# A third expert weight buffer and 32-row tiles in the mixture-of-experts half of a fused decoder layer

## What is computed

```python
x = x + g1 * y                                  # after the mixer: "x2" in the kernel
h = rms_norm(x, norm_ffn) * (1 + sc2) + sh2
x = x + g2 * hier_moe(h, ...)                   # "x3" in the kernel
return rms_norm(x, final_norm)
...
# hier_moe: 4 groups of 4 experts; each token takes the top group and the top 2 experts in it
g_top  = top_k(softmax(t @ w_rg + b_rg), 1)
e_top  = top_k(softmax(logits_e of that group), 2)
for each expert:                                # w_gate, w_up: 1024 x 512, w_down: 512 x 1024
    hid = silu(t @ w_gate) * (t @ w_up)
    y  += combine[:, expert] * (hid @ w_down)
```

## Time and profile before

| | |
|---|---|
| median of 3 runs | 833.36 us (833.19 to 833.53) |
| the profiled execution, its own time | 836.89 us |
| its span in the trace | 835.2 us |
| PE busy | 702.7 us, 84% of the span |
| DVE, ACT, POOL busy | 335.3, 177.6, 131.2 us |
| moved by DMA | 173.49 MB, mean 208 GB/s |

### The profile page before, as it was taken

How to read it: one execution, slowest core, us unless ns; L and a number is a source line. 1 busy time by engine, 2 the same in 40 slices (tenths; PEclk the granted TensorE clock), 3 DMA queues, 4 the chain that set the end, 5 groups by cost and what they waited for, 6 DMA issues and landing times.

```text
span 835.2 us, 8861 instructions
## 1 busy us (share of the span) xinstructions
PE 702.7 (84%) x3377; PEld 397.4 (48%) x3377; DVE 335.3 (40%) x743; ACT 177.6 (21%) x427; POOL 131.2 (16%) x171
## 2 busy tenths in 40 slices
PE   0469899999999998889999815999998999899920
PEld 0455445667675796555544513444443344334300
DVE  4932566866575434867221174011211111021107
ACT  3203225121121213557121201111211112011103
POOL 8650022313050281000000001000000000000021
PEclk9669999999999998989999855999999999999975
DMA  9899802222220305510520422489999999999935
GB/s 335 262 312 276 288 0 101 101 102 101 101 101 1 53 1 192 191 73 2 202 94 19 168 97 64 165 281 401 374 388 396 381 399 383 399 369 397 398 110 230
DMA packets 88092, 173.49 MB, mean 208 GB/s; under 512 B 19347, under 2 KB 23533, under 8 KB 88045
## 3 DMA queue, kind: packets, MB, share of 16 engines
q1 hardware_dynamic: 78048, 151.12, 50.8%
q0 software_dynamic: 4240, 15.21, 5.6%
q10 hardware_dynamic: 5756, 6.52, 2.3%
HBM read 157.63 MB, written 15.20 MB: 207 GB/s over the span
## 4 chain that ended last, share of the span: by engine, by line
PE 66%; DVE 14%; DMA 12%; ACT 3%; issue 2%; POOL 1%; SPq 0%; ACTq 0%; POOLq 0%; DVEq 0%
PE ps L962 14%; DMA gu<-in_w_up 10%; PE ps L1067 7%; PE ps L2107 6%; PE ps L2074 5%; PE ps L955 3%; PE ps L989 3%; DVE acc L1733 3%; PE ps L2185 2%; PE ps L2191 2%; PE ps L2071 2%; PE ps L983 2%; PE ps L2098 2%; PE ps L2195 2%; PE ps L636 1%
## 5 line engine op out<-in xcount | busy, mean ns | idle before, releaser
L962 PE MATMUL ps<-gu,xgT 128*128 128x512 f32 x256 | 117.0, 617 | 8.3 <-DMA gu<-in_w_up 5.9
L962 PEld LDWEIGHTS ps<-gu,xgT 128*128 128x128 f32 x256 | 49.9, 198 | 70.5 <-issue 63.7
L1401 POOL DMA_INDIRECT xg<-xn_rows,list x16 | 15.0, 940 | 413.1 <-PE ps L943 221.2
L2107 PE MATMUL ps<-hT,winr 128*128 128x512 f32 x144 | 72.1, 609 | 0.0
L1733 DVE SCALAR_TENSOR_TENSOR acc<-ada,st,acc 128x512 f32<-128x512 f32 x84 | 68.1, 811 | 2.3
L1067 PE MATMUL ps<-wout,yT 128*128 128x512 f32 x128 | 58.6, 617 | 0.0
L955 PE MATMUL ps<-gu,xgT 128*64 128x512 f32 x256 | 56.7, 595 | 0.0
L989 PE MATMUL ps<-dn,hidT 128*128 128x512 f32 x128 | 56.5, 594 | 0.0
L1038 DVE TENSOR_TENSOR hidm<-sg,ps 128x512 f32<-128x512 f32 x8 | 5.5, 686 | 121.6 <-ACT sg L1005 121.6
L1587 POOL TENSOR_TENSOR cc<-low,lev 128x512 f32<-128x512 f32 x20 | 30.2, 1520 | 129.7 <-DVE low L1919 104.2
L2074 PE MATMUL ps<-hT,wind 128*128 128x512 f32 x96 | 42.3, 593 | 0.0
(11 more groups left out here) (401 smaller groups left out, 1041.9 us busy)
## 6 DMA issues: line engine op xcount, KB each, us to landing
gu<-in_w_gate SPq DMA_DIRECT2D x16, 2048.0 KB, 14.6
gu<-in_w_up SPq DMA_DIRECT2D x16, 2048.0 KB, 20.5
dn<-in_w_down SPq DMA_DIRECT2D x16, 2048.0 KB, 20.5
ada<-in_w_ada SPq DMA_DIRECT2D x12, 2048.0 KB, 10.4
expert_rows<-zero POOLq DMA_DIRECT2D x9, 512.0 KB, 10.8
expert_rows<-yo ACTq DMA_DIRECT2D x8, 512.0 KB, 6.7
wout<-in_w_out SPq DMA_DIRECT2D x1, 3072.0 KB, 10.7
x<-in_x SPq DMA_DIRECT2D x2, 1024.0 KB, 6.2
```

The costliest lines, as they stand in the source:

```text
L962: ins = nc.tensor.matmul(PS[2 * b + w][:, :], T["xgT"][:, k, :], gu[b][:, w, k, :], start=(k == 0), stop=(k == KT - 1))
L2107: ins = t.matmul(bank[:, :], w(k), T["hT"][:, k, :], start=(k == 0), stop=(k == KT - 1))
```

## The change

- A third pair of weight buffers, `gu2` and `dn2`. `gu2` lies over the old x, xn2, x2T, `g1b`, `g2b` and `fnb`, and `dn2` over x2. Experts 0, 1 and 2 are now pinned, and step n uses buffer n % 3.
- x2 is therefore stored to a DRAM tensor `x2_rows` after the output projection (4 stores of 512 KB) and loaded again near the end as `x3` (2048 KB), over `dn1`. `fnb`, the final norm's gains, is loaded near the end too.
- g2 is copied to places of its own (`g2m`, `g2s`, `g2q`) by ACT, ahead of the routing's two exponentials; before, DVE made `g2s`, after the routing.
- The tiles are now 8 of 128 rows, 4 of 64 and 4 of 32. In a 32-row tile four products of 32 rows run side by side, each against a quarter of the weights' columns (moving size 256), with their results in four groups of 32 partitions.
- The order of ranks is now 0, 1, 2, 15, 3, 14, 4, 13, 5, 12, 6, 11, 7, 8, 9, 10.
- `EXTRA` goes from 9 to 12, with as many DRAM tiles zeroed by POOL near the start. Several semaphores of the routing are merged into one that counts.

```diff
-EXTRA = 9
-BIG = 8
-HALF = 64
+EXTRA = 12
+NBUF = 3
+SIZES = [128] * 8 + [64] * 4 + [32] * 4
...
     at("x2", R1 + 64 * K + 256, [P, ST, D])
+    at("dn2", R1 + 64 * K + 256, [P, FT, D])
+    at("x3", RW + 16 * K, [P, ST, D])
...
+    at("gu2", RX, [P, 2, KT, F])
...
-    ORDER = [0, 1]
-    for m in range(BIG - 2):
-        ORDER += [BIG + m, 2 + m]
-    ORDER += [E - 2, E - 1]
+    ORDER = list(range(NBUF))
+    big, less = list(range(NBUF, BIG)), list(range(BIG, E))
+    rest = less[::-1] if NBUF == 3 else less
+    while big:
+        ORDER.append(rest.pop(0))
+        ORDER.append(big.pop(0))
+    ORDER += rest[::-1] if NBUF == 3 else rest
@@ sync_moe
-        sp.dma_start(T["fnb"][:], A["final_norm"].partition_broadcast(P)).then_inc(sem("fn_in"), 16)
-        sp.wait_ge(sem("experts"), 1)
+        for i in range(ST):
+            sp.dma_start(x2_d[i * P:(i + 1) * P, :], T["x2"][:, i, :]).then_inc(sem("x2_st"), 16)
+        sp.wait_ge(sem("g2_moved"), 1)
+        sp.wait_ge(sem("ss"), 2 * ST)
+        sp.wait_ge(sem("logit_mm"), ST)
+        for b in range(2):
+            sp.wait_ge(sem(f"xn2_st{b}"), 32)
+        load_gate_up(sp, 2, 2)
+        sp.wait_ge(sem("x2_st"), 16 * ST)
+        load_down(sp, 2, 2)
+        sp.wait_ge(sem("routing"), ROUTING["experts"])
...
-        for n in range(2, E + 1):
+        for n in range(NBUF, E + 1):
...
-                sp.wait_ge(sem("gu_mm"), n - 1)
-                load_gate_up(sp, expert[n], n % 2)
-            if n >= 3:
-                sp.wait_ge(sem("dn_mm"), n - 2)
-                load_down(sp, expert[n - 1], (n - 1) % 2)
+                sp.wait_ge(sem("gu_mm"), n - NBUF + 1)
+                load_gate_up(sp, expert[n], n % NBUF)
+            if n > NBUF:
+                sp.wait_ge(sem("dn_mm"), n - NBUF)
+                load_down(sp, expert[n - 1], (n - 1) % NBUF)
+        sp.wait_ge(sem("gu_mm"), E - 1)
+        sp.dma_start(T["fnb"][:], A["final_norm"].partition_broadcast(P)).then_inc(sem("fn_in"), 16)
+        sp.wait_ge(sem("dn_mm"), E - 2)
+        sp.dma_start(T["x3"][:], x2_d.rearrange("(i p) d -> p i d", p=P)).then_inc(sem("x3_in"), 16)
@@ pe_gate_up, a tile of fewer than 128 rows (pe_down alike)
+            parts = P // m
+            f = F // parts
             for k in range(KT):
-                for s in range(2):
+                for s in range(parts):
                     ins = nc.tensor.matmul(
-                        PS[2 * b][HALF * s:HALF * s + HALF, :].rearrange("p (w f) -> p w f", w=2),
-                        T["xgT"][:, k, 0:HALF], gu[b][:, :, k, s * GW:(s + 1) * GW], start=(k == 0),
-                        stop=(k == KT - 1))
+                        PS[2 * b][m * s:m * s + m, 0:2 * f].rearrange("p (w f) -> p w f", w=2),
+                        T["xgT"][:, k, 0:m], w_in[:, :, k, s * f:(s + 1) * f], start=(k == 0), stop=(k == KT - 1))
@@ act_moe, ahead of the exponentials
+        act.wait_ge(sem("oproj_mm"), ST)
+        act.wait_ge(sem("ada_out"), HPS - 4)
+        for name, m in (("g2m", P), ("g2s", 64), ("g2q", 32)):
+            d = D * m // P
+            for s in range(P // m):
+                ins = a.activation(T[name][m * s:m * s + m, :], T["g2b"][m * s:m * s + m, s * d:(s + 1) * d], ACT.Copy)
+        ins.then_inc(sem("g2_moved"), 1)
@@ dve_moe, in the routing
-        link(v.tensor_scalar(t16, order, -float(BIG), 0.0, ALU.add, ALU.max))
         link(v.tensor_scalar(tile0, order, float(P), None, ALU.mult))
-        v.scalar_tensor_tensor(tile0, t16, -float(P - HALF), tile0, ALU.mult, ALU.add)
-        link(v.tensor_scalar(pad, order, BIG - 0.5, float(P - HALF), ALU.is_gt, ALU.mult))
+        for m, n in enumerate(STEPS_DOWN):
+            less = float(SIZES[n - 1] - SIZES[n])
+            link(v.tensor_scalar(t16, order, -float(n), 0.0, ALU.add, ALU.max))
+            link(v.scalar_tensor_tensor(tile0, t16, -less, tile0, ALU.mult, ALU.add))
+            if m:
+                link(v.tensor_scalar(t16, order, n - 0.5, less, ALU.is_gt, ALU.mult))
+                link(v.tensor_tensor(pad, pad, t16, ALU.add))
+            else:
+                link(v.tensor_scalar(pad, order, n - 0.5, less, ALU.is_gt, ALU.mult))
...
-        link(v.scalar_tensor_tensor(e16[:], rank, float(HALF), pad.unsqueeze(1).broadcast_to([P, ST, E]), ALU.is_ge,
-                                    ALU.mult))
+        wide_pad = pad.unsqueeze(1).broadcast_to([P, ST, E])
+        link(v.tensor_tensor(e16[:], rank, wide_pad, ALU.add))
+        link(v.scalar_tensor_tensor(e16[:], e16[:], float(P), wide_pad, ALU.is_ge, ALU.mult))
...
-        v.tensor_copy(T["g2s"][0:HALF, :], T["g2b"][0:HALF, 0:512])
-        v.tensor_copy(T["g2s"][HALF:P, :], T["g2b"][HALF:P, 512:1024])
@@ dve_moe, at the end
         dve.wait_ge(sem("fn_in"), 16)
+        dve.wait_ge(sem("x3_in"), 16)
```

More of the change, by code:

```diff
@@ L48 @@
 FT = F // P
-EXTRA = 9
-BIG = 8
-HALF = 64
-TILE_START = [P * n for n in range(BIG)] + [P * BIG + HALF * n for n in range(E - BIG)]
-TILE_START += [P * BIG + HALF * (E - BIG) + P * n for n in range(EXTRA)]
+EXTRA = 12
+NBUF = 3
+ROUTING = {"chosen": 1, "places": 2, "slots": 3, "list": 4, "experts": 5, "w12": 6, "route_i": 7}
+ROUTING_PE = {"rank_mm": 1, "list_mm": 2}
+SIZES = [128] * 8 + [64] * 4 + [32] * 4
+TILE_START = [sum(SIZES[:n]) for n in range(E + 1)]
+TILE_START += [TILE_START[E] + P * (n + 1) for n in range(EXTRA - 1)]
 ROWS = TILE_START[-1] + P
+BIG = SIZES.count(P)
+STEPS_DOWN = [n for n in range(1, E) if SIZES[n] < SIZES[n - 1]]
 EPS = 1e-6
@@ L940, in pe_rows @@
             pe.wait_ge(sem("xgT_d"), n)
-        m = HALF if small(n) else P
+        m = rows_of(n)
         for k in range(KT):
@@ L968, in pe_hidden, with pe_down @@
         pe.wait_ge(sem("hidm"), n + 1)
-        for f in range(2 if small(n) else FT):
+        for f in range(FT * rows_of(n) // P):
             ins = nc.tensor.transpose(PS[2 * b][:, f * P:(f + 1) * P], T["hidm"][:, f * P:(f + 1) * P], idf[:])
         ins.then_inc(sem("hid_tr"), 1)
-    def pe_down(pe, n, b, came):
+    def pe_down(pe, n):
+        w_in = dn[buffer_of(n)]
         pe.wait_ge(sem("hidT"), n + 1)
-        pe.wait_ge(sem(f"dn_in{b}"), came)
+        pe.wait_ge(sem(f"dn_in{buffer_of(n)}"), 16 * loads_of(n))
         pe.wait_ge(sem("yo_d"), n + 1)
+        m = rows_of(n)
         if small(n):
+            parts = P // m
+            per = FT // parts
+            d = D // parts
             for f in range(FT):
[L981 to L984, removed]
-                                           dn[b][:, f, w * 512:(w + 1) * 512], start=(f == 0), stop=(f == FT - 1))
+                s, c = f // per, f % per
+                for w in range(parts):
+                    ins = nc.tensor.matmul(PS[4][m * w:m * w + m, 0:d], T["hidT"][:, c, m * s:m * s + m],
+                                           w_in[:, f, w * d:(w + 1) * d], start=(f == 0), stop=(f == FT - 1))
         else:
@@ L1016, in act_output @@
         start = TILE_START[ORDER[n] if n < E else n]
-        rows = yo_d[start:start + (HALF if small(n) else P), :]
-        if small(n):
-            for s in range(2):
-                act.dma_start(rows[:, s * 512:(s + 1) * 512], T["yo"][HALF * s:HALF * s + HALF, 0:512]
-                              ).then_inc(sem("yo_st"), 16)
-        else:
-            act.dma_start(rows, T["yo"][:]).then_inc(sem("yo_st"), 16)
+        m = rows_of(n)
+        d = D * m // P
+        for s in range(P // m):
+            act.dma_start(yo_d[start:start + m, s * d:(s + 1) * d], T["yo"][m * s:m * s + m, 0:d]
+                          ).then_inc(sem("yo_st"), 16)
     def dve_rows(dve, n):
         dve.wait_ge(sem("xg_tr"), n + 1)
-        m = HALF if small(n) else P
+        m = rows_of(n)
         for k in range(4, KT):
@@ L1135, in pe_moe @@
                                start=(n + i == 0), stop=(n == 1 and i == ST - 1))
-        ins.then_inc(sem("list_mm"), 1)
-        pe.wait_ge(sem("list"), 1)
+        ins.then_inc(sem("routing_pe"), 1)
+        pe.wait_ge(sem("routing"), ROUTING["list"])
         pe_rows(pe, 0, 0, 16)
-        pe_gate_up(pe, 0, 0, 32)
+        pe_gate_up(pe, 0, 0)
         pe_rows(pe, 1, 1, 16)
@@ L1392, in pool_moe @@
         at = bass.IndirectOffsetOnAxis
-        pool.wait_ge(sem("list"), 1)
+        pool.wait_ge(sem("routing"), ROUTING["list"])
         for b in range(2):
@@ L1530, in _ @@
         link(g.tensor_scalar(T["pinned"][:], T["e1"][:], -1.0, float(E - 1), ALU.mult, ALU.add))
-        for e in range(2):
-            link(g.memset(T["pinned"][:, e:e + 1], (2 - e) * 1e6))
+        for e in range(NBUF):
+            link(g.memset(T["pinned"][:, e:e + 1], (NBUF - e) * 1e5))
         pool.wait_ge(sem("masks"), 1)
```

105 lines of the change are left out of this document (62 added, 43 removed).

## The result

The changed kernel takes **823.42 us** (median of 4 runs, 822.75 to 825.09) against 833.44 (833.19 to 835.39) for the kernel before on the same chip: a ratio of 0.9865 (95% interval 0.9834 to 0.9895), 10.0 us less. The forecast was 817.5 in a range of 812 to 826: the direction and the range held, and in the main the mechanism, and the gain is 10 us where 15.9 were forecast. The profiled execution of the changed kernel took 824.05 us, with a span of 822.1, against 836.89 and 835.2 before.

A forecast was written before the change was run, and what follows sets the result against it. Before the change DMA and PE were full together, after it the weights' stream alone; 793.4 - 19.6 + 1.6 + 1.2 = 776.6 for the last down load, last down ending at 784.2, execution 821.0, median 817.5 us, range 812 to 826.

The forecast's parts named there:

- first rival: 32-row steps: four products side by side don't overlap, a step costs 11.4 us, PE stays full; about 826, chance 0.05.
- The account of bytes: Weights' stream: 98.8 MB before, 91.2 MB after, 7.6 MB less, at 388 GB/s 19.6 us less.
- The late loads: Loads of x2, gu2 and dn2 before the first gather: if late, they share its engines, 0 to 3 us; 0 taken.
- The other rivals: Holes in the stream, about 828 (0.07); slower clock after waits, about 847 (0.04); a spare tile used, about 856 (0.01).
- A change that relieves one of the two gains almost nothing: Expert loop before the change: DMA and PE are full together, so relieving only one gains almost nothing.
- check of PE's chain for the kernel before: PE's step times summed from 516.0 with eight steps of 11.6 and its waits give 800; its last down ended at 800.5.
- The stretch to the last gate/up: From the first load into a freed buffer to the last gate/up's start: 19.4 us less.
- The new hole: Stream: step 5's load waits for a 128-row gate/up until 570.4 us; costs about 1.6 us, bounds 0 and 5.
- Step 0: Routing chain ahead of step 0 and the stream's start: more linked operations, 1.2 us more.
- The last gate/up: Last gate/up to end of last down: 16.5 us before, 1.9 us added for the clock's fall after a wait.
- The 32-row step: PE's work on a 32-row tile: 1.9 + 1.0 + 1.0 for transposes, 3.9 us a step, other bound 11.4.
- Waits in nearly every pair: Expert loop: PE waits some 10 us for weights per pair of a 128- and a 32-row expert; a sign of being right.

The follow-up runs named there:

- The buffer alone: The changed kernel with tiles of 8 x 128 and 8 x 64 rows as before; third buffer, x2 through memory and order stay: 826.88 us, ratio 0.9897.
- second execution: The changed kernel run again with no edit, against the kernel before on the same chip: 823.72 us, ratio 0.9868.
- the three kernels with the other order: The changed kernel with 32-row tiles in the last two steps: 820.97 us; with gate half freed early and spare tiles' work later: 816.32; plus useless products: 817.21.

## Why the prediction was right, and where 6 us went

**What held, and what the number owes to luck.** 823.4 lies in the forecast's own range of 813 to 824, but nearer to the first rival's 826 than to 817.5; the time alone would not have told the two apart. The traces do: a 32-row gate/up takes 3.66 us and not 7, and PE has slack. The account of bytes said that the weights' stream would bound the kernel alone. The DMA share is 1.04 to 781 us with PE busy for 93% of the time, and taking 4.2 MB away brought the last gate/up 11.1 us forward, for the 10.7 us that they need. The late loads are out too: `xg` of step 0 was there 4.4 us after its gather was issued, and 5.4 before. The other rivals are out: 32-row steps are cheap, no load after 576 us came late enough to open a hole, the waits did not halve the clock for long, and there were 16 steps.

**"A change that relieves one of the two gains almost nothing" was wrong.** The buffer alone gains 8.6 us. Both resources were full on average, but PE lost time at particular places, in waits for weights and slow stretches behind them, and in that run these are gone. That it is the 6.3 MB loaded ahead that removes them, and not the third place or the order, is likely but not shown. The forecast's own rival had this sum in it (about 826, PE full without waits), and 826.88 is what the buffer alone gives; the general sentence above it ignored it. In the check of PE's chain for the kernel before, the forecast's named terms give 796.4; only with those two slow stretches of 1.7 us each do they reach the 800 that it states.

**The stretch to the last gate/up: -15.1 for -19.4.** This is the term that was mis-sized, by 4.3 us.
- The new hole was foreseen at its place (570.4; the load went out at 569.00) but costs some 3.7 us and not 1.6. The stretch from 567 to 576 us moved 0.110 x 4 + 0.324 x 5 = 2.06 MB, where 391 GB/s would have moved 3.5: 3.7 us. Only the first bytes' delay of one load, 1.5 us, was counted. But the bytes in flight ran out at about 567.8, 1.2 us before that load went out, and the stream was back only some 2 us after it, as two short windows show; the 5 us behind the hole then ran at 324 GB/s.

```profile
567.50:568.00 0.50, 0.50 (x3) 0.26 (x2) 0.00 (x0) 0.00 (x0) 0.00 (x0) 1.00 0.61 246
...
571.00:571.50 0.50, 0.50 (x2) 0.19 (x1) 0.06 (x1) 0.00 (x0) 0.00 (x0) 1.00 0.76 254
```

- 0.39 MB of the saved bytes are step 3's gather (rank 15 has 32 rows, where 128 stood), ahead of the hole at 544 us. What is saved ahead of a hole only makes the hole longer: 1.0 us that the account booked as gain.
- When the last gate/up weights landed, 0.74 MB of the loads behind them had already moved, 1.9 us. The forecast let the loads finish one after the other.
- The stream ran at 391 GB/s instead of 388: 1.6 us to the good. About 1 us remains unplaced, as much as this stretch differs between executions of the changed kernel (236.9, 235.9, 236.5).

The experiment that frees the gate half early all but closes the holes and starts the stream earlier, and 3.9 us come back.

**Step 0: +1.9 for +1.2.** The routing chain took 1.6 us more (35.6 to 37.2 from SP's issue of `dn` 0 and 1 to `list`), gate/up 0 took 1.0 us more, and 0.7 came back between them, because the first gather landed 1.0 us sooner. The 1.0 us is no cost of the change: the changed kernel's gate/up 0 took 15.86 us in its second execution, as before. In that execution the whole stretch is 62.5 us, 0.9 more than before and not 1.9. DVE's work for three more spare tiles was taken as covered, 0.4 without cover; where DVE released gate/up 0, it came 0.1 to 0.3 us late.

**The last gate/up: +2.3 for +1.9.** It begins behind a wait of 5.9 us. The window of the changed kernel over that place (PEclk is third from the end):

```profile
765.00:770.00 5.00, 2.77 (x8) 0.91 (x10) 0.00 (x0) 0.00 (x0) 0.00 (x0) 0.50 1.03 411
```

The granted clock is at its lower level, 1.2 GHz, and the gate/up takes 9.27 us instead of 7.09. The Trainium skill (TensorE: Matmul & The Clock Gate, HAM oscillation) describes this fall behind waits for DMA. The trace agrees, with one difference in weight: only the last of the four waits had a price in the end time; another, behind 4.87 us, made a gate/up of 128 rows take 16.15 us instead of 13.9, and that was swallowed by the slack, since PE waited for weights again two steps later.

**The tail: +1.4 for +0.45.** The three `If`s are there, at 0.15 us each. The rest was not in the sum: the last store took 3.40 us to land (2.90 before) and the gather of y 6.24 (5.88). It comes back in the other traces of the same tail: from the end of the last down to the end of the span are 36.0 and 36.3 us in the changed kernel's other two executions, and 36.6 with the third buffer alone. Why it is longer stays open, and for the kernel before there is only one trace.

**The 32-row step was mis-sized, without effect.** The low end was taken and halved rightly, but from the wrong count. A 64-row tile makes 8 x 2 gate/up products and a 32-row one 8 x 4, and the trace records each of these float32 products twice: 32 of 512 columns in 7.0 us, and 64 of 256, at 57 ns each. So gate/up takes 3.66 us and not 1.9, down 1.93 and not 1.0, and a pair of a 128- and a 32-row step 28.4 us of PE and not 26.0. It still lies under the 35.8 us that the pair's weights take, so the end did not move. The Trainium skill (TensorEngine Tiling (Array Packing), Theoretical Speedup) gives up to four times for 32. The trace agrees: 13.90 us for 128 rows to 3.66 are 3.8 times.

**"Waits in nearly every pair" was wrong.** There were four, the first at about 673 us. The stream starts with three experts in the buffers, and PE, which is slower than forecast by 2.4 us a pair, needs until then to use up that lead.

## What to carry to other kernels

When two resources are full over the same stretch, ask where each loses time, and not only how full it is: relieving one can remove the waits that it caused on the other. A byte saved ahead of a hole in a stream is worth nothing, so an account by bytes is made from the last hole on, and each hole is priced from the time the bytes in flight run out to the time the stream is back, not from the issue alone. At the end of a stream-bound loop the smallest tile belongs last, and the last load sets the floor; whether a second `yo` buffer would give back what its product waited was not run. And before a change of 1 us in one trace is put down to an edit, a second trace of the unedited kernel should be read: gate/up 0 differed by that much without any.

## What the runs showed of the hardware

- A group of 32 recorded products of the output projection with nothing to wait for took 16.60 us in one execution and 13.98 in another of the same code. The mean granted clock from 400 to 440 us was 0.93 of full speed in one and 1.00 in the other. That group alone moved one span by 2.6 us. In three of the other traces the group behind it took 15.68 us.
- Products without a use that fill a wait of PE up to its last 0.75 us kept the clock up: 7.09 us for the gate/up behind it, and 9.39 without them. Where 2.31 us of waiting were left behind them, a 32-row gate/up took 5.35 us, between the 3.66 of full clock and the 6.00 without them.
- With four products of 32 rows side by side, an expert's gate/up on 32 rows takes 3.66 us where 128 rows take 13.90: a quarter of the rows in 1/3.8 of the time, at 57 ns for each recorded product of 256 columns.
- The loads held 391 GB/s over 205 us at a DMA share of 1.04.
- Small stores were not slower to land in themselves. For the step before the last, with the loads still running, four of 32 rows took 5.0 to 5.2 us and two of 64 rows 5.5; for the last step, four of 32 rows took 2.8 to 3.7 us in the three kernels with the other order, and two of 64 rows 2.9 to 3.6.
